# A streaming-encoder step on one core: the order of work at the end of the HGRN levels and around the expert gather

## The chip, the cores and the metric
One Trainium2 chip, one of its cores. The metric is the device time of one execution in microseconds, median of several runs; lower is better. All data are float32.

## What is computed
One layer over 320 tokens, 256 of a prompt and 64 of a sample, model width 2048. In short, with `h = adaLN(RMSNorm(x))`:
```
proj = h @ w_in                        # split into z, xbc, dt, hq, hf, hi, hgate, u
A: Mamba-2 SSD      B: HGRN2 (4 heads, key 128, value 128)      C: S5 diagonal SSM
x += gt1 * (concat(A, B, C) @ w_out)
x += gt2 * hmoe(adaLN(RMSNorm(x)))     # top-1 group, top-2 of its 8 experts, 32 experts of width 256
y = RMSNorm(x)
```
The part that the first half of the change touches is the chunkwise gated recurrence of B, in chunks of 64 tokens:
```
b = cumsum(log f)                       # in the chunk
intra = (q . k . exp(b_t - b_s), s <= t) @ v
inter = (q * exp(b)) @ S
kd = k * exp(b_last - b)
S = S * exp(b_last) + kd^T @ v
```
The second half sits where `hmoe` starts: router logits, top-1 group, softmax weights, and rows of `h` fetched for each expert.

## The kernel before
Five engines run own instruction streams, tied by semaphores; every step is laid out by hand, and within an engine all is in order. A list PLAN, made at build time by `make_plan` (line 75), gives TensorE its order; ScalarE and VectorE walk ACT_PLAN, the same list with slightly moved items.

**First 610 us.** TensorE multiplies `w_in` (17 chunks of 256 columns behind the first three, each 2 MB, two groups of 16 matmuls, line 1101) and `w_ada` (line 1000). SyncE loads the chunks into a ring of four slots as TensorE frees them (line 417). Between these "bulk" groups stand the small steps of S5 and of HGRN. HGRN takes two heads at once (hp = 0, 1). `hg_prep` makes log f and its running sum `hb`. Then seven levels: in level 0 the diagonal, in levels 1 to 6 blocks of 32 down to 1 tokens. A level is two subtractions into `hE` on VectorE (lines 1840, 1841), an exponential on ScalarE (line 799), two products into `hq_` and `hk_` (lines 1844, 1845), 12 small matmuls (line 1207) and, one level later, a masked sum into `hAT` by `hg_take` (lines 1828, 1830).

Behind the levels stands `hg_kd` (lines 801 and 1847). VectorE takes the last level's scores with `hg_take(hp, 6)`, sets a small element as a signal (line 1850), ScalarE writes exp(b) over `hE` (line 803), VectorE makes `hq_ = q * exp(b)` (line 1852), copies the last column of each chunk (line 1854), writes b_last - b into `hE` (line 1855), ScalarE takes its exponential (line 805), VectorE multiplies by k (line 1857), and TensorE turns the result (line 1219). For hp = 0 the plan has on TensorE: level 6, `ada 19,0`, the turning, `in 14,1`. For hp = 1: level 6, `in 18,0`, the turning, `ada 23,0`. On VectorE, between level 6 and `hg_kd(0)`, stands a convolution step (lines 1926, 1928), and on ScalarE the taking of a group of `in 14` out of PSUM (lines 743, 744). `hg_state` and `hg_out` (line 1234) follow, the latter with `hq_` as an operand.

**610 to 805 us.** SSD, the output projection (lines 1134, 1388), the second norm.

**805 to 860 us.** ScalarE makes h (line 702), TensorE the logits (line 1403), and turns h back into rows in 12 groups of four transposes (line 1418; PSUM banks 4 to 7, so a group from the fifth on needs the copy four before it). VectorE runs the routing in some 30 tiny steps (2095 to 2139), hands `rt_expo` over at 2133, then makes the mask `Mk` (2139) that TensorE ranks (line 1426; behind the twelve groups in its order), takes the ranks (2150 to 2157), lets TensorE place tokens (1434) and writes the row numbers `slot_rows` (2165). ScalarE waits for `rt_expo`, does two small exponentials (917, 918), copies the twelve groups (924), then stores all rows of h to DRAM in two transfers (928, 929). GpSimd waits for `slot_rows` and the stores, then gathers the rows of the first pair of experts (634). TensorE turns these (1450), VectorE copies them (2197), and `hidden(0)` starts (1463).

**860 to 1366 us.** 16 pairs of experts. SyncE loads gate and up weights in halves as TensorE is done with a half (line 459), 12 MB a pair in all with the down weights; VectorE, ScalarE and TensorE form the activation and the down product (1487). Then the rows are gathered, weighed, normed and stored.

Of the kernel before, what the change touches and what calls it, by code (L numbers as in the profile page):

```python
# [24 lines left out]
P = 128  # L25
# [3 lines left out]
T = TP + TS  # L29
# [156 lines left out]
def build(nc, a, o):  # L186

    ctx = ExitStack()
    with ctx:
# [70 lines left out]
        hAT = ar(2944, 384)  # L260
        vn = ar(3328, 768).rearrange("p (h q k) -> p h q k", h=2, q=3)
# [231 lines left out]
        def _(pool):  # L493
# [128 lines left out]
            pool.wait_ge(S("h2_stored"), 32)  # L622
# [28 lines left out]
        def _(act):  # L651
# [144 lines left out]
            def hg_level(hp, lv):  # L796
                if lv:
                    act.wait_ge(S("hg_expo"), 6 * hp + lv)
                    st(s.activation(hE, hE, ACT.Exp), "hg_exp")

            def hg_kd(hp):
                act.wait_ge(S("hg_expo2"), 2 * hp + 1)
                st(s.activation(hE, hb, ACT.Exp), "hg_exp2")
                act.wait_ge(S("hg_expo2"), 2 * hp + 2)
                st(s.activation(hE, hE, ACT.Exp), "hg_exp2")
# [110 lines left out]
            act.wait_ge(S("rt_expo"), 1)  # L916
            st(s.activation(rt[:, 16:28], rt[:, 16:28], ACT.Exp))
            st(s.activation(rt[:, 240:243], rt[:, 240:243], ACT.Exp), "rt_exp")

# [7 lines left out]
            act.wait_ge(S("act_rows"), 12)  # L927
            act.dma_start(h2_dram[0:TP].rearrange("(j p) d -> p j d", p=P), hn[:, 0:2, :]).then_inc(S("h2_stored"), 16)
            act.dma_start(h2_dram[TP:T], hn[0:TS, 2, :]).then_inc(S("h2_stored"), 16)
# [49 lines left out]
        def _(pe):  # L979
# [6 lines left out]
            pe.wait_ge(S("setup_taken"), 1)  # L986
            def sum_squares(b, count, tag):
                for i in range(count):
                    pe.wait_ge(S("squares"), NORM[tag] + i + 1)
                    for q in range(2):  # L990
                        last = mm(bank(b, T), ones[:, :], sq[:, i % 2, q * T:q * T + T],
                                  start=(i == 0 and q == 0), stop=(i == count - 1 and q == 1))
                    last.then_inc(S("squares_used"), 1)
# [198 lines left out]
            def hg_level(hp, lv):  # L1192

                it = 7 * hp + lv
                if lv == 0:
                    pe.wait_ge(S("hg_k"), hp + 1)
                    q_, k_ = (flat[:, (x + 2 * hp) * T:(x + 2 * hp + 2) * T] for x in (HQ, HF))
                else:
                    pe.wait_ge(S("hg_qk"), 6 * hp + lv)
                    q_, k_ = hq_, hk_  # L1200
# [33 lines left out]
            def hg_out(hp):  # L1234
                pe.wait_ge(S("hg_S"), NCH * (hp + 1))
                pe.wait_ge(S("hg_sc_used"), 7 * (hp + 1))

# [272 lines left out]
            pe.wait_ge(S("act_rows"), 12)  # L1510
            for g_ in range(4):
                turn_x(0, g_, 0)
# [68 lines left out]
        def _(dve):  # L1581
# [265 lines left out]
            def hg_kd(hp):  # L1847
                q_, k_ = (flat[:, (x + 2 * hp) * T:(x + 2 * hp + 2) * T] for x in (HQ, HF))
                hg_take(hp, 6)
                st(v.memset(small[:, 60:61], 0.0), "hg_expo2")  # L1850
                dve.wait_ge(S("hg_exp2"), 2 * hp + 1)
                st(tt(hq_, q_, hE, MUL))
                e3, b3 = (t.rearrange("p (n r) -> p n r", r=CH) for t in (hE, hb))
                st(v.tensor_copy(small[:, 80:90].unsqueeze(2), e3[:, :, CH - 1:CH]))
                st(tt(e3, bc(b3[:, :, CH - 1:CH], [P, 10, CH]), b3, SUB), "hg_expo2")
                dve.wait_ge(S("hg_exp2"), 2 * hp + 2)
                st(tt(hE, k_, hE, MUL), "hg_kd")
                for h in range(2):
                    dve.wait_ge(S("hg_kd_turned"), 2 * hp + h + 1)
                    b4 = bank(6 + h, 384).rearrange("p (q k) -> p q k", q=3)  # L1860
                    st(v.tensor_copy(kdn[:, h, 0:2, :], b4[:, 0:2, :]))
                    st(v.tensor_copy(kdn[0:64, h, 2, :], b4[0:64, 2, :]), "hg_kdn" if h else None)
# [337 lines left out]
            dve.wait_ge(S("h2_stored"), 32)  # L2200
# [128 lines left out]
```

## Time and profile before

| | |
|---|---|
| median of 3 runs | 1426.47 us (1426.3 to 1431.44) |
| the profiled execution | 1419.03 us, of which its span 1417.2 us |
| mean granted TensorE clock of the span | 0.925 |
| TensorE busy | 1186.0 us, 84% of the span |
| VectorE, ScalarE, GpSimd busy | 517.5, 195.9, 260.9 us |
| chain that ended last | PE 47%, DMA 27%, DVE 9%, POOL 9% |

The profile is of one execution. PE is TensorE, PEld its weight loads, DVE VectorE, ACT ScalarE, POOL GpSimd, SP SyncE. "L1219" is line 1219 of the kernel. "x32" counts instructions; one float32 matmul is two of them. "[4.14 <-DVE mem L1857]" is idle time of the engine ahead of the row and what ended it. The granted clock is a share of 2.4 GHz; it is 1.00 or 0.50 (1.2 GHz), and values between are means over a stretch.

### The profile page before, as it was taken

What the parts mean: (1) busy time and instruction counts of PE and PEld (TensorE: products, weight loads), DVE (VectorE), ACT (ScalarE), POOL (GpSimd) and SP (SyncE); (2) the same over time, 40 slices, a digit from 0 to 9 for tenths busy, and PEclk for the clock granted to TensorE, in tenths of its full rate; (3) what the DMA queues carried; (4) which work ended last, traced back from release to release, by engine and by line L of the source; (5) the groups of instructions that cost most, each with busy time, mean ns of one, the idle gap of its engine ahead of it and who ended that gap; (6) DMA issues with size and microseconds to landing.
All of it is one profiled execution on the core that took longest, in us unless ns stands there. A gap on an engine that the chain in (4) does not pass through costs nothing.

```text
span 1417.2 us, 14773 instructions
## 1 busy us (share of the span) xinstructions
PE 1186.0 (84%) x5922; PEld 641.6 (45%) x5922; DVE 517.5 (37%) x991; ACT 195.9 (14%) x319; POOL 260.9 (18%) x568
## 2 busy tenths in 40 slices
PE   4789999998998899989989868878878888877840
PEld 2345555654565565656657543323333333333310
DVE  2412476565454464435642362111112111111208
ACT  1302110100211311232210140000000000000003
POOL 4070188884000000011120000100000000010010
PEclk9899999999999899979999988998999999999975
DMA  9999477765766467432223446999999999999934
GB/s 338 374 351 366 144 272 261 273 228 195 236 232 227 142 234 262 154 95 89 90 75 119 152 160 235 418 421 420 412 416 397 405 402 411 402 410 400 420 155 133
DMA packets 140086, 387.02 MB, mean 273 GB/s; under 512 B 15211, under 2 KB 54501, under 8 KB 112558
## 3 DMA queue, kind: packets, MB, share of 16 engines
q1 hardware_dynamic: 132208, 361.91, 67.7%
q0 software_dynamic: 6528, 18.72, 3.8%
q10 hardware_dynamic: 1280, 5.42, 1.1%
q8 instruction: 49, 0.80, 0.2%
q14 instruction: 21, 0.17, 0.0%
HBM read 385.95 MB, written 23.13 MB: 289 GB/s over the span
## 4 chain that ended last, share of the span: by engine, by line
PE 47%; DMA 27%; DVE 9%; POOL 9%; SPq 3%; issue 3%; ACT 2%; POOLq 0%; DVEq 0%; ACTq 0%
DMA slot<-in_w_exp_up 22%; PE psum L1101 11%; PE psum L1463 11%; PE psum L1134 5%; PE psum L1388 5%; DMA slot<-in_w_ada 3%; PE psum L1000 3%; PE psum L1030 3%; POOL mem L558 1%; POOL sq L556 1%; POOL sq L559 1%; POOL mem L561 1%; POOL sq L560 1%; POOL sq L557 1%; SPq L443 1%
## 5 line engine op out<-in xcount | busy, mean ns | idle before, releaser
L1463 PE MATMUL psum<-slot,mem 128*64 128x512 f32 x1024 | 256.0, 659 | 66.8 <-DMA slot<-in_w_exp_up 65.9
L1101 PE MATMUL psum<-hT,slot 128*128 128x320 f32 (+1 forms) x1056 | 298.5, 442 | 0.0
L1101 PEld LDWEIGHTS psum<-hT,slot 128*128 128x128 f32 (+1 forms) x1056 | 199.0, 191 | 96.7 <-issue 21.5
L1463 PEld LDWEIGHTS psum<-slot,mem 128*64 128x64 f32 x1024 | 81.9, 151 | 232.0 <-issue 156.6
L2207 DVE TENSOR_TENSOR sq<-sq,psum 128x256 f32<-128x256 f32 x16 | 6.7, 422 | 328.1 <-ACT sq L935 328.1
L1487 PE MATMUL psum<-mem,sq 128*64 128x512 f32 x512 | 113.4, 595 | 8.3 <-issue 6.6
L1000 PE MATMUL psum<-slot,cT 128*8 128x512 f32 (+1 forms) x768 | 103.0, 647 | 20.7 <-DMA slot<-in_w_ada 20.7
L628 POOL DMA_INDIRECT moe_output<-mem,idx x16 | 16.2, 1010 | 481.8 <-ACT mem L939 481.8
L1134 PE MATMUL psum<-mem,slot 128*128 128x320 f32 x256 | 76.9, 458 | 0.0
L1388 PE MATMUL psum<-mem,slot 128*128 128x320 f32 x256 | 71.1, 441 | 5.4 <-DVE mem L2022 5.4
L1487 PEld LDWEIGHTS psum<-mem,sq 128*64 128x64 f32 x512 | 42.0, 137 | 69.5 <-issue 67.9
L1388 PEld LDWEIGHTS psum<-mem,slot 128*128 128x128 f32 x256 | 49.7, 195 | 26.4 <-issue 6.5
L1134 PEld LDWEIGHTS psum<-mem,slot 128*128 128x128 f32 x256 | 50.5, 201 | 24.6 <-issue 7.1
L935 ACT ACTIVATE sq<-psum 128x256 f32<-128x256 f32 x16 | 6.1, 383 | 340.2 <-PE psum L1463 340.2
L1450 PE MATMUL psum<-ident,mem 128*128 128x128 f32 x256 | 38.4, 285 | 17.4 <-DVE mem L2197 9.0
L1000 PEld LDWEIGHTS psum<-slot,cT 128*8 128x8 f32 (+1 forms) x768 | 17.3, 90 | 73.0 <-issue 67.9
L2197 DVE COPY mem<-psum 128x512 f32<-128x512 f32 x64 | 42.5, 684 | 9.5 <-PE psum L1450 9.5
L1450 PEld LDWEIGHTS psum<-ident,mem 128*128 128x128 f32 x256 | 29.1, 145 | 33.2 <-issue 30.9
L939 ACT ACTIVATE mem<-psum 128x1024 f32<-128x1024 f32 x16 | 16.4, 1023 | 161.8 <-PE psum L1487 161.8
L2220 DVE COPY mem<-psum 128x1024 f32<-128x1024 f32 x16 | 19.6, 1224 | 51.9 <-PE psum L1487 51.9
L634 POOL DMA_INDIRECT mem<-moe_input,idx x16 | 16.4, 1026 | 119.5 <-DMA moe_input<-mem 115.0
L1030 PE MATMUL psum<-hT,mem 128*128 128x320 f32 x128 | 37.3, 442 | 1.3 <-ACT hT L702 1.3
(448 smaller groups left out, 1259.7 us busy)
## 6 DMA issues: line engine op xcount, KB each, us to landing
slot<-in_w_ada SPq DMA_DIRECT2D x48, 2048.0 KB, 10.7
slot<-in_w_exp_gate SPq DMA_DIRECT2D x64, 1024.0 KB, 13.3
slot<-in_w_exp_up SPq DMA_DIRECT2D x64, 1024.0 KB, 16.4
mem<-in_w_exp_down SPq DMA_DIRECT2D x32, 2048.0 KB, 17.5
slot<-in_w_in SPq DMA_DIRECT2D x17, 2048.0 KB, 11.8
slot<-in_w_out SPq DMA_DIRECT2D x8, 2048.0 KB, 8.0
mem<-in_w_in SPq DMA_DIRECT2D x2, 2048.0 KB, 18.0
mem<-in_x_prompt ACTq DMA_DIRECT2D x1, 2048.0 KB, 12.1
```

Source lines behind the costliest of these rows:

```text
L634: pool.indirect_dma_start(xg[i % 2], None, h2_dram, bass.IndirectOffsetOnAxis(ap=slot_rows[:, i:i + 1], axis=0), bounds_check=T - 1, oob_i ...
L939: s.activation(ys[:, 1024:2048], psum[:, 3:5, :].rearrange("p b n -> p (b n)"), ACT.Copy)\
L1000: done = mm(psum[32 * c:32 * c + width, 2, :], cT[:, 8 * h + kk, lo:lo + width], w[:, kk, :], start=(first and kk < 4), stop=(last and kk ...
L1030: last = mm(bank(EARLY_BANK[e], T), w[:, k, q * P:(q + 1) * P], hT[:, k, :], start=(k == 0), stop=(k == KD - 1))
L1101: last = mm(psum[0:wd, grp % 2, 0:T], w[:, k, q * P:q * P + wd], hT[:, k, :], start=(k == 0), stop=(k == KD - 1))
L1134: last = mm(bank(grp % 2, T), w[:, k, q * P:(q + 1) * P], mixed[8 + k], start=(k == 4), stop=(k == 3))
L1388: last = mm(bank(4 + m % 4, T), w[:, k, q * P:(q + 1) * P], mixed[k], start=(k == 0), stop=(k == 7))
L1450: last = tr(bank(6 + g_ % 2, P, lo=q * P), xg[par][:, (4 * g_ + q) * P:(4 * g_ + q + 1) * P], ident[:, :])
L1463: last = mm(psum[rows_, 0, :].rearrange("p (w n) -> p w n", w=2), xe[i % 2][:, k, rows_], gate_up[h][:, :, k, :], start=(k == 0), stop=(k ...
L1487: last = mm(psum[rows_, 1 + n, :], aTT[:, f, rows_], dn[h][:, f, 512 * n:512 * n + 512], start=(f == 0), stop=(f == 1))
L2197: v.tensor_copy(xe[par][:, 4 * g_:4 * g_ + 4, :], bank(6 + g_ % 2).rearrange("p (k t) -> p k t", k=4))\
L2220: v.tensor_copy(ys[:, 0:1024], psum[:, 1:3, :].rearrange("p b n -> p (b n)")).then_inc(S("y_left"), 1)
```

## The change
In HGRN, exp(b) gets a buffer of its own, `hX`, and is made in level 2. In `hg_kd`, b_last - b is formed at once, and the take of level 6 and `q * exp(b)` come behind the decayed keys; `hg_qk` counts seven steps for each hp instead of six, and `hg_out` waits for the seventh. At the gather, the two exponentials of the gate move behind the twelve copies; each tile of rows is stored as soon as its four copies are done, in three transfers; and TensorE runs 18 matmuls of constants (`idle_work`) into bank 4 ahead of the turning of the first gathered rows.
```diff
+        hX = ar(7168, 640)
...
-            pool.wait_ge(S("h2_stored"), 32)
+            pool.wait_ge(S("h2_stored"), 48)
...
+                if lv == 2:
+                    if hp:
+                        act.wait_ge(S("hg_qk"), 7 * hp)
+                    st(s.activation(hX, hb, ACT.Exp), "hg_exp2")
 
             def hg_kd(hp):
-                act.wait_ge(S("hg_expo2"), 2 * hp + 1)
-                st(s.activation(hE, hb, ACT.Exp), "hg_exp2")
-                act.wait_ge(S("hg_expo2"), 2 * hp + 2)
+                act.wait_ge(S("hg_expo2"), hp + 1)
                 st(s.activation(hE, hE, ACT.Exp), "hg_exp2")
...
-            act.wait_ge(S("rt_expo"), 1)
-            st(s.activation(rt[:, 16:28], rt[:, 16:28], ACT.Exp))
-            st(s.activation(rt[:, 240:243], rt[:, 240:243], ACT.Exp), "rt_exp")
-
             for g_ in range(12):
...
-            act.wait_ge(S("act_rows"), 12)
-            act.dma_start(h2_dram[0:TP].rearrange("(j p) d -> p j d", p=P), hn[:, 0:2, :]).then_inc(S("h2_stored"), 16)
-            act.dma_start(h2_dram[TP:T], hn[0:TS, 2, :]).then_inc(S("h2_stored"), 16)
+                if kg == 3:
+                    act.wait_ge(S("act_rows"), g_ + 1)
+                    act.dma_start(h2_dram[j * P:j * P + n], hn[0:n, j, :]).then_inc(S("h2_stored"), 16)
+            act.wait_ge(S("rt_expo"), 1)
+            st(s.activation(rt[:, 16:28], rt[:, 16:28], ACT.Exp))
+            st(s.activation(rt[:, 240:243], rt[:, 240:243], ACT.Exp), "rt_exp")
...
+            def idle_work(b, count):
+
+                for _ in range(count):
+                    mm(bank(b, P), ones[:, :], ident[:, :], start=True, stop=True)
...
-                    pe.wait_ge(S("hg_qk"), 6 * hp + lv)
+                    pe.wait_ge(S("hg_qk"), 7 * hp + lv)
...
                 pe.wait_ge(S("hg_sc_used"), 7 * (hp + 1))
+                pe.wait_ge(S("hg_qk"), 7 * (hp + 1))
...
             pe.wait_ge(S("act_rows"), 12)
+            idle_work(4, 18)
...
-                hg_take(hp, 6)
-                st(v.memset(small[:, 60:61], 0.0), "hg_expo2")
+                e3, b3, x3 = (t.rearrange("p (n r) -> p n r", r=CH) for t in (hE, hb, hX))
+                st(tt(e3, bc(b3[:, :, CH - 1:CH], [P, 10, CH]), b3, SUB), "hg_expo2")
                 dve.wait_ge(S("hg_exp2"), 2 * hp + 1)
-                st(tt(hq_, q_, hE, MUL))
-                e3, b3 = (t.rearrange("p (n r) -> p n r", r=CH) for t in (hE, hb))
-                st(v.tensor_copy(small[:, 80:90].unsqueeze(2), e3[:, :, CH - 1:CH]))
-                st(tt(e3, bc(b3[:, :, CH - 1:CH], [P, 10, CH]), b3, SUB), "hg_expo2")
+                st(v.tensor_copy(small[:, 80:90].unsqueeze(2), x3[:, :, CH - 1:CH]))
                 dve.wait_ge(S("hg_exp2"), 2 * hp + 2)
                 st(tt(hE, k_, hE, MUL), "hg_kd")
+                hg_take(hp, 6)
+                st(tt(hq_, q_, hX, MUL), "hg_qk")
...
-            dve.wait_ge(S("h2_stored"), 32)
+            dve.wait_ge(S("h2_stored"), 48)
```

## Rows read from the trace of the kernel before

**Rows 1.** The page, busy time, share of the span, instructions.
```profile
PE 1186.0 (84%) x5922; PEld 641.6 (45%) x5922; DVE 517.5 (37%) x991; ACT 195.9 (14%) x319; POOL 260.9 (18%) x568
```
**Rows 2.** Windows, the expert stage: length, busy by engine (instructions), clock, DMA share, GB/s.
```profile
900.00:1300.00 400.00, 327.84 (x1510) 130.76 (x1512) 69.62 (x110) 16.89 (x24) 24.33 (x24) 0.92 1.00 410
```
**Rows 3.** The chain that ended last, in order of time: start, length, what.
```profile
859.17 13.97 PE psum L1463 x64
...
1348.37 8.81 PE psum L1463 x32
```
**Rows 4.** Waits of TensorE, 440 to 860 us, the longest: total, times, longest.
```profile
PE psum L1450 <- DMA mem<-moe_input,idx: 6.9, 1, 6.9
```
**Rows 5.** Timeline, end of the HGRN levels of hp = 0.
```profile
435.00 1.28 DVE L1928 SCALAR_TENSOR_TENSOR mem<-mem,parT,sq 128x256 f32<-128x256 f32 x4
...
438.26 0.22 ACT L744 ACTIVATE mem<-psum 128x64 f32<-128x64 f32 x1
438.52 1.90 PE L1000 MATMUL psum<-slot,cT 128*8 128x512 f32 x16
...
440.02 0.74 ACT L803 ACTIVATE mem<-mem 128x640 f32<-128x640 f32 x1 [1.54 <-DVE small L1850]
...
443.68 0.83 DVE L1857 TENSOR_TENSOR mem<-mem 128x640 f32<-128x640 f32 x1 [0.93 <-ACT mem L805]
...
444.56 1.42 PE L1219 MATMUL psum<-ident,mem 128*128 128x128 f32 x6 [4.14 <-DVE mem L1857]
```
**Rows 6.** The chain in order of time, around both turnings of the decayed keys.
```profile
445.99 9.74 PE psum L1101 x32
...
551.82 8.81 PE psum L1101 x32
560.63 0.65 PE psum L1219 x6
```
**Rows 7.** Timeline of ScalarE behind the exponential of level 2, hp = 1.
```profile
521.19 0.74 ACT L799 ACTIVATE mem<-mem 128x640 f32<-128x640 f32 x1 [7.85 <-DVE mem L1841]
```
**Rows 8.** Timeline, row turning and routing.
```profile
827.47 1.97 PE L1418 MATMUL psum<-ident,hT 128*128 128x128 f32 x16
...
833.79 2.56 ACT L924 ACTIVATE mem<-psum 128x512 f32<-128x512 f32 x5
...
834.53 5.01 PE L1418 MATMUL psum<-ident,hT 128*128 128x128 f32 x32 [5.10 <-ACT mem L924]
...
835.35 0.26 DVE L2139 TENSOR_TENSOR sq<-sq 128x96 f32<-128x96 f32 x1
...
840.70 0.23 DVE L2150 COPY sq<-psum 128x64 f32<-128x64 f32 x1 [3.06 <-PE psum L1426]
...
846.78 0.18 DVE L2165 CAST idx<-mem 128x32 uint32<-128x32 f32 x1
...
847.14 0.59 PE L1439 MATMUL psum<-mem,ones 128*128 128x3 f32 x2 [1.13 <-DVE mem L2166]
```
**Rows 9.** The chain in order of time, store and gather.
```profile
840.83 8.42 DMA moe_input<-mem
...
850.18 4.28 DMA mem<-moe_input,idx
...
854.60 1.94 PE psum L1450 x8
```
**Rows 10.** Timeline, TensorE at full clock: eight transposes; eight 128-column matmuls.
```profile
873.06 1.09 PE L1450 MATMUL psum<-ident,mem 128*128 128x128 f32 x8
...
1105.87 2.05 PE L1507 MATMUL psum<-ident,modT 128*128 128x128 f32 x16
```
**Rows 11.** Windows of 1 us around the gather, columns as in Rows 2.
```profile
837.00:838.00 1.00, 1.00 (x10) 1.00 (x9) 0.57 (x3) 0.74 (x3) 0.00 (x0) 0.87 0.00 0
...
844.00:845.00 1.00, 1.00 (x8) 0.85 (x8) 0.00 (x0) 0.00 (x0) 0.00 (x0) 0.55 0.94 393
...
857.00:858.00 1.00, 1.00 (x8) 0.96 (x6) 0.48 (x2) 0.00 (x0) 0.00 (x0) 0.63 0.00 0
```

## The prediction
> **What bounds the kernel now.** First the page: TensorE is busy for 84% of the span, the others far less [rows 1]. That is an average, so I read it by stage. In the expert stage, 900 to 1300 us, TensorE is busy for 328 of 400 us while the DMA engines are at a share of 1.00 and 410 GB/s [rows 2]: there the weights set the pace. The chain in order of time says when this begins. `hidden(0)` starts at 859.17, and the first weights of the next pair are asked for when its first half is done, 7 us later; the last half ends at 1357.2 [rows 3]. So work ahead of 859.17 can still be saved, and what is saved there moves the whole transfer stage; inside it nothing is gained by a faster TensorE.
>
> Ahead of it, the list of TensorE's waits between 440 and 860 us is what to look at: no transfer of weights is in it, and its longest is for the gathered rows, 6.9 us [rows 4]. The timeline has the two stalls that the change aims at. At the end of the levels of hp = 0 TensorE waits 4.14 us for the decayed keys [rows 5]; around the routing it waits 5.10 us for ScalarE's first row copies [rows 8], and the store and gather follow in the chain [rows 9].
>
> **Decayed keys, hp = 0.** TensorE is done with `ada 19,0` at 438.52 + 1.90 = 440.42 and turns the keys only at 444.56 [rows 5]. The chain between is: take of level 6, signal, exp(b) at 440.02, product, last columns, difference, exponential, product with k at 443.68. After the change the difference needs only `hb`, so VectorE makes it when the convolution ends, at 436.3 [rows 5]. ScalarE takes its exponential behind the PSUM copies that end at 438.26 + 0.22 = 438.48; with 0.74 each for the exponential [rows 5] and 0.05 of handing over it is done at 439.3. The product, 0.83, is done at 440.2, ahead of the 440.42. The margin is 0.2 us, thin but positive. Saved: 444.56 - 440.42 = 4.1 us.
>
> The stall also costs clock. With it, turning and the next group take 1.42 + 9.74 = 11.2 us; for hp = 1, where TensorE does not wait, the turning takes 0.65 and a like group 8.81, together 9.5 [rows 5, 6]. So 1.7 us more, and 5.8 us in all. The bounds of this term are 4.1 (the clock falls anyway) and 5.8.
>
> What goes behind the keys is hidden: take, sum and `q * exp(b)` are about 2 us of VectorE and must be done before `hg_out`; the copies of the turned keys come 1 us behind the turning and TensorE has a group of 8.81 us [rows 6] ahead of `hg_state`. If that group were not there, these 2 us would show. For hp = 1 TensorE passes from the group to the turning without a gap, 551.82 + 8.81 = 560.63 [rows 6], so nothing is to be had: 0. The additional exponential, 0.74 for each hp, is issued behind level 2's own; ScalarE's next work there comes after 7.85 us of idling [rows 7]: 0. Its wait for `hg_qk` (hp = 1) is met long before; behind it in the queue stands only the next PSUM copy. `hg_out`'s new wait is met ahead of the group that TensorE does before `hg_state`: 0. The signal and its hand-over go too, on no path that is left.
>
> **Gate exponentials behind the row copies.** Now the first four groups are turned at 827.47 + 1.97 = 829.44, but ScalarE copies only from 833.79, when `rt_expo` has come, and TensorE's other eight run from 834.53 to 839.54 [rows 8]. The ranking stands behind them, so VectorE, with its next operand ready, idles 3.06 us until 840.70 [rows 8]. After the change the copies start at 828.1, take 12 x 0.51 (2.56 for five [rows 8]) and two issues of about 0.5, and the turnings end at about 834. `Mk` is there at 835.35 + 0.26 = 835.6 [rows 8], the ranking takes a good microsecond, and VectorE goes on when its own work is done, at 837.64. Saved on the routing chain: 3.0 us; `slot_rows` comes at 843.96 instead of 846.96. Next in line is VectorE itself, so no more than 3.06 is to be had. The exponentials, with a table load, come at about 836 to 838; their reader, VectorE's weights, stands at 848 - 3 = 845. Behind ScalarE's wait for `rt_expo` stands only the first SiLU of the experts: 0.
>
> **Rows stored by tile.** Now 2 MB and behind them 0.5 MB are issued; the latter, issued at 840.83, lands 8.42 later, at 849.25; the gather starts at 850.18, 0.93 behind it [rows 9]. In the new order the stores are issued at about 830.7, 833.2 and 835.9, when the DMA engines are idle (share 0.00 [rows 11]). Were the last to take the whole 8.42 us, it would land at 844.3; with a fifth of the bytes left it will be well ahead of the 843.96. So the row numbers come last: gather at 843.96 + 0.93 = 844.9, landed 4.28 later [rows 9], TensorE could turn at 849.3. Against 854.60 [rows 9] that is 5.3 us. The third issue costs ScalarE 0.5 us, hidden under the wait for `Mk`.
>
> **Constant matmuls.** TensorE's last small step ends at 847.14 + 0.59 = 847.73 [rows 8], so at 844.7 in the new order, and the 18 matmuls start there. Their price is not in the stage, but eight matmuls of this shape take 2.05 us at full clock [rows 10], 0.256 each, 4.6 for 18: till 849.3, just when the rows land. At half clock eight transposes take 1.94 against 1.09 [rows 9, 10], a ratio of 1.78, so 0.456 each and 8.2 us: till 852.9. Which clock? Before the change TensorE resumed at 834.53 and the second 837 to 838 reads 0.87; it resumed at 854.60 and 857 to 858 reads 0.63 [rows 8, 9, 11]. As only 0.50 and 1.00 occur, the rises are at 837.3 and 857.7, 2.7 and 3.1 us after the work resumed. Short bursts did not hold it: it fell at about 844.1 amid work (0.55 [rows 11]). The new order has such pauses too, so I take 2.9 us at half clock (6.4 matmuls) and 11.6 x 0.256 = 3.0 at full: 5.9 us, till 850.6. The filler then holds the turning by 1.3 us (bounds 0 and 3.6).
>
> The Trainium skill ("TensorE: Matmul & The Clock Gate", Part 1, "Wait — 56ns, not 53.3ns?") has back-to-back matmuls of 128 columns at 107 ns with the array cold and 56 warm, a ratio of 1.9. By it an all-cold filler would be an estimated 8.8 us, the hold 4.2 instead of 3.6, and the sum 0.6 less in that case; it speaks for the first rival below, and the trace's 1.78 roughly agrees.
>
> What it buys: the turning runs at full clock, 8 transposes 0.85 us faster [rows 9, 10]. Turning to `hidden(0)` took 859.17 - 854.60 = 4.57; it will take 3.7. So `hidden(0)` starts at 850.6 + 3.7 = 854.3: 4.9 us earlier (bounds 1.7, all half: 852.9 + 4.57 = 857.5; and 6.2, all full: 849.3 + 3.7 = 853.0).
>
> **Sum.** 5.8 + 4.9 = 10.7 us. The profiled execution took 1419.03 (span 1417.2 and 1.8 around it): 1408.3. It is 7.4 us below the median of the runs shown, 1426.47; nothing in the change depends on where those 7.4 lie, so I take the same saving off the median: 1415.8. A measurement of this kernel can tell about 0.5%, 7.1 us, from no change.
>
> **Rival 1: the filler holds the rows.** It runs at half clock throughout and TensorE, in order, turns at 852.9. For it: 844 to 845 reads 0.55 just where the clock would be needed [rows 11]. Against: the filler is itself gapless work, and both rises came within 3.1 us of such. 5.8 + 1.7 = 7.5: 1419.0, at the edge of what can be told.
>
> **Rival 2: the HGRN gain is given back.** TensorE comes 5.8 us earlier to each later step up to 805 us; if a load of the ring or a partner engine has its own time, the stall reappears there. Against: no weight transfer in 420 us of waits [rows 4]; the partners start from TensorE's own results. For: a margin of only 0.2 us at the keys. Then 4.9 are left: 1421.6, no change.
>
> **Rival 3, slower: TensorE becomes the bound of the expert stage.** It has 400 - 328 = 72 us of room in 400 [rows 2], over 12 pairs 6 us a pair. The new start shifts its waits against the clock's falls; should it run at half clock for over 6 us of work more in each pair (mean clock from 0.92 to about 0.75), each pair is drawn out. One microsecond a pair over 15 pairs costs 15: 1426.5 - 10.7 + 15 = 1430.8. It decides from 0.7 us a pair. For it: the clock is below 1 in the stage already. Against: the pattern of waits is made by the transfers and returns in each pair.
>
> **How the numbers follow.** Forecast 0.66, rival 1 0.14, rival 2 0.14, rival 3 0.04, both parts without effect 0.02. The forecast's own bounds are 4.1 + 4.9 = 9.0 and 5.8 + 6.2 = 12.0, so 1414.5 to 1417.5. Three executions of the old kernel lie 5 us apart, so below I go to 1410; above, the range takes in rivals 1 and 2: 1422. Faster by over 0.5% (below 1419.3): 0.66 and half of rival 1, 0.73. Within 0.5%: the other half, rival 2 and the 0.02, 0.23. Slower: 0.04.
>
> **What would show it.** In the new profile: TensorE turns the keys of hp = 0 directly behind `ada`, with no wait at L1219 and the group behind it at 8.81; the copies at L924 start within 1 us of the first turning; VectorE's wait ahead of the ranks is gone; the gather starts under 1.2 us behind `slot_rows` and not behind a store; clock rises inside the filler; `hidden(0)` starts 10 to 11 us earlier and the DMA stage keeps its length. I am wrong if the filler ends over 2 us behind the landing of the rows, if TensorE shows a new wait between 440 and 805 us, or if the expert stage grows.

## Result and profile after

| | before | after |
|---|---|---|
| median, six runs each | 1427.33 us (1426.01 to 1431.44) | 1415.11 us (1410.4 to 1420.39) |
| ratio, 95% interval | | 0.9924 (0.9907 to 0.9941) |
| profiled execution: span | 1417.2 us | 1408.6 us |
| mean granted clock | 0.925 | 0.922 |

The kernel is faster by 0.76%, 10.8 us by the ratio, with an interval of 2.4 us to either side; the two medians lie 12.2 us apart. The forecast was 1415.8 in place of 1426.47, 10.7 us. The span of the profiled execution went down by 8.6.

What bounds the kernel is as before. The page of the changed kernel, busy time of each engine, answers to [rows 1]:

```profile
PE 1190.3 (85%) x5958; PEld 644.9 (46%) x5958; DVE 517.0 (37%) x989; ACT 195.8 (14%) x319; POOL 261.4 (19%) x568
```
The window of the expert stage of the changed kernel, columns as in [rows 2]:
```profile
890.00:1290.00 400.00, 325.70 (x1508) 130.51 (x1506) 70.12 (x110) 17.29 (x25) 24.37 (x24) 0.91 1.00 410
```

The DMA share is 1.00 and the rate 410 GB/s in both, so the gain should lie ahead of the stage. At the keys of hp = 0 the chain in order of time of the changed kernel (start, length, what) has no wait left; compare [rows 5, 6]:

```profile
438.72 1.83 PE psum L1008 x16
440.55 0.81 PE psum L1227 x6
441.36 8.62 PE psum L1109 x32
```

L1227 is the turning, formerly L1219. The timeline of the changed kernel (start, busy time, engine, line) shows why it is not late: the difference (L1860) is formed when the convolution ends, the exponential (L808) behind ScalarE's copies, the product (L1864) ends 0.3 us before the turning.

```profile
436.43 0.83 DVE L1860 TENSOR_TENSOR mem<-mem 128x640 f32<-128x640 f32 x1
...
438.51 0.73 ACT L808 ACTIVATE mem<-mem 128x640 f32<-128x640 f32 x1
...
439.34 0.83 DVE L1864 TENSOR_TENSOR mem<-mem 128x640 f32<-128x640 f32 x1 [1.87 <-ACT mem L808]
...
440.49 0.87 PE L1227 MATMUL psum<-ident,mem 128*128 128x128 f32 x6
```

The routing, in the timeline of the changed kernel, answers to [rows 8, 9]:

```profile
821.68 3.71 PE L1427 MATMUL psum<-ident,hT 128*128 128x128 f32 x32
...
822.38 2.07 ACT L923 ACTIVATE mem<-psum 128x512 f32<-128x512 f32 x4 [4.87 <-PE psum L1427]
...
829.44 0.49 ACTq L928 DMA_DIRECT2D moe_input<-mem  x1
...
831.89 0.22 DVE L2159 COPY sq<-psum 128x64 f32<-128x64 f32 x1
...
834.14 3.73 PE L1443 MATMUL psum<-rows,sq 128*64 128x32 f32 x24 [2.50 <-DVE sq L2166]
...
838.64 0.18 DVE L2174 CAST idx<-mem 128x32 uint32<-128x32 f32 x1
...
839.45 6.49 PE L993 MATMUL psum<-ident,ones 128*128 128x128 f32 x36
...
839.71 1.12 POOL L635 DMA_INDIRECT mem<-moe_input,idx  x1 [110.83 <-DVE mem L2175]
...
845.78 1.04 PE L1459 MATMUL psum<-ident,mem 128*128 128x128 f32 x8
```

ScalarE copies (L923) 0.7 us behind the first turning; VectorE takes the ranks (L2159) without the idling of 3.06 us; the gather (POOL L635) is released by VectorE's row numbers, not by a store; the filler (L993) ends when TensorE turns (L1459). `hidden(0)` starts at 849.4 against 859.2.

Executions differ by up to 4 us in when they reach the levels of hp = 0, so from here on I compare lengths of stretches, each the difference of two starts read from the timelines. The **lead** is from the last small matmul of level 6 to the turned keys; the **middle** from there to the last logits matmul (the last of the small ones that turn the logits and add their bias, L1408 before, L1417 after); the **gather** from that matmul to the first weight load of the second pair; the **rest** from that load to the end of the span. The column "rows" is when VectorE starts to write the row numbers, counted from the last logits matmul. For before: `hidden(0)` at 31.85 and the load 7.12 later, 38.97.

| kernel | lead | middle | rows | gather | rest |
|---|---|---|---|---|---|
| before | 6.19 | 382.76 | 19.46 | 38.97 | 550.9 |
| after | 1.98 | 381.05 | 17.11 | 35.00 | 552.1 |
| hgrn_only | 1.98 | 385.86 | 19.47 | 38.98 | 552.3 |
| gather_only | 6.19 | 385.69 | 17.11 | 35.48 | 551.9 |
| no_fill | 1.98 | 385.93 | 17.11 | 35.97 | 552.2 |
| fill36 | 1.98 | 380.48 | 17.10 | 39.05 | 552.5 |
| two_stores | 1.98 | 380.47 | 17.10 | 35.03 | 552.4 |
| exps_first | 1.98 | 387.08 | 21.32 | 38.83 | 550.9 |
| take_first | 4.10 | 384.04 | 17.11 | 35.47 | 552.4 |
| clock_hold | 6.19 | 385.30 | 21.32 | 41.85 | 551.4 |
| spread_fill | 1.98 | 385.75 | 15.77 | 32.19 | 555.4 |
| more_fill | 1.98 | 377.50 | 15.84 | 31.97 | 555.0 |
| silu_early | 1.99 | 383.86 | 17.11 | 35.00 | 550.4 |
| more_fill_silu | 1.98 | 378.18 | 15.84 | 32.02 | 551.5 |

Of the kernels whose time is not told below, one execution each: `fill36` 1414.06, `two_stores` 1412.72, `exps_first` 1420.39, `take_first` 1417.16, `clock_hold` 1424.06; executions of one kernel lie up to 13 us apart (`before`: 1421.9 to 1434.6 in 20), so their verdicts rest on the stretches alone.

From before to after: -4.2 in the lead, -1.7 in the middle, -4.0 in the gather, +1.2 in the rest and +0.1 in the start, together -8.6. A single middle is a poor witness, though: in the kernels that turn the keys at 1.98 and have no filler in the middle it lies anywhere from 380.5 to 387.1. That goes with the granted clock. Summed over the middle, TensorE was at 0.50 for 51 us in `before`, `after`, `fill36` and `two_stores` (middles of 380.5 to 382.8), for 58 us in `hgrn_only`, `gather_only`, `no_fill`, `spread_fill` and `silu_early` (383.9 to 385.9), and for 65 us in `exps_first` (387.1); `take_first` and `clock_hold` lie between, with 55 us (384.0) and 61 us (385.3). The -1.7 of this one pair of profiles is therefore no measure of what the change did to the clock. That is why the parts were timed as well.

### The profile page after: what moved, and what is told of

It reads as the page before. It is cut to its first block, busy times and chain, and to the rows that moved or that the text cites. A ratio compares the mean times of both kernels' runs of the same rounds, so it can differ in the third digit from the quotient of the medians.

```text
span 1408.6 us, 14842 instructions
## 1 busy us (share of the span) xinstructions
PE 1190.3 (85%) x5958; PEld 644.9 (46%) x5958; DVE 517.0 (37%) x989; ACT 195.8 (14%) x319; POOL 261.4 (19%) x568
## 4 chain that ended last, share of the span: by engine, by line
PE 49%; DMA 26%; DVE 9%; POOL 9%; SPq 3%; issue 3%; ACT 2%; POOLq 0%; DVEq 0%; ACTq 0%
DMA slot<-in_w_exp_up 21%; PE psum L1109 11%; PE psum L1472 11%; PE psum L1397 5%; PE psum L1142 5%; DMA slot<-in_w_ada 3%; PE psum L1008 3%; PE psum L1038 3%; PE psum L1496 2%; POOL mem L559 1%; DMA mem<-in_w_exp_down 1%; POOL sq L557 1%; POOL sq L560 1%; POOL mem L562 1%; POOL sq L561 1%
## 5 line engine op out<-in xcount | busy, mean ns | idle before, releaser
L1008 PE MATMUL psum<-slot,cT 128*8 128x512 f32 (+1 forms) x768 | 103.5, 650 | 20.8 <-DMA slot<-in_w_ada 20.8
L1008 PEld LDWEIGHTS psum<-slot,cT 128*8 128x8 f32 (+1 forms) x768 | 17.2, 90 | 73.0 <-issue 68.1
L1459 PE MATMUL psum<-ident,mem 128*128 128x128 f32 x256 | 37.1, 278 | 13.2 <-DVE mem L2206 10.9
L1459 PEld LDWEIGHTS psum<-ident,mem 128*128 128x128 f32 x256 | 27.9, 140 | 29.0 <-issue 25.7
L635 POOL DMA_INDIRECT mem<-moe_input,idx x16 | 16.5, 1028 | 115.4 <-DVE mem L2175 110.8
## 6 DMA issues: line engine op xcount, KB each, us to landing
slot<-in_w_ada SPq DMA_DIRECT2D x48, 2048.0 KB, 10.2
slot<-in_w_in SPq DMA_DIRECT2D x17, 2048.0 KB, 11.7
```

The source lines that it names most:

```text
L635: pool.indirect_dma_start(xg[i % 2], None, h2_dram, bass.IndirectOffsetOnAxis(ap=slot_rows[:, i:i + 1], axis=0), bounds_check=T - 1, oob_i ...
L1008: done = mm(psum[32 * c:32 * c + width, 2, :], cT[:, 8 * h + kk, lo:lo + width], w[:, kk, :], start=(first and kk < 4), stop=(last and kk ...
L1459: last = tr(bank(6 + g_ % 2, P, lo=q * P), xg[par][:, (4 * g_ + q) * P:(4 * g_ + q + 1) * P], ident[:, :])
```

## Experiments

### The two parts alone
`hgrn_only` has the HGRN part of the diff and the old gather; `gather_only` the reverse.
```diff
 hgrn_only, against the changed kernel
+            act.wait_ge(S("rt_expo"), 1)
+            st(s.activation(rt[:, 16:28], rt[:, 16:28], ACT.Exp))
+            st(s.activation(rt[:, 240:243], rt[:, 240:243], ACT.Exp), "rt_exp")
             for g_ in range(12):
...
-                if kg == 3:
-                    act.dma_start(h2_dram[j * P:j * P + n], hn[0:n, j, :]).then_inc(S("h2_stored"), 16)
...
+            act.dma_start(h2_dram[TP:T], hn[0:TS, 2, :]).then_inc(S("h2_stored"), 16)
...
-            idle_work(4, 18)
 gather_only, against the changed kernel
-                    st(s.activation(hX, hb, ACT.Exp), "hg_exp2")
...
+                st(s.activation(hE, hb, ACT.Exp), "hg_exp2")
...
+                hg_take(hp, 6)
+                st(v.memset(small[:, 60:61], 0.0), "hg_expo2")
+                dve.wait_ge(S("hg_exp2"), 2 * hp + 1)
+                st(tt(hq_, q_, hE, MUL))
...
                 st(tt(hE, k_, hE, MUL), "hg_kd")
-                hg_take(hp, 6)
-                st(tt(hq_, q_, hX, MUL), "hg_qk")
```


> The HGRN part of the change alone; gate exponentials, stores and gather as in the kernel before, no constant matmuls. Theory 1 (the two parts add up: 5.8 us at the keys of hp = 0, 4 us at the gather): TensorE turns the keys directly behind ada, hidden(0) starts near 859.2 - 5.8 = 853.4, the time is 0.996 of before (1421.5 against 1427.3). Theory 2 (the HGRN gain is given back before the expert stage and all of the gain is the gather's): hidden(0) at 859 +- 0.5, ratio 1.000.

> The gather part alone; HGRN as in the kernel before. Theory 1: the wait of 4.1 us at the keys is back, hidden(0) starts 4.0 us earlier than before, at 855.2, ratio 0.997. Theory 2 (the gather brings all): hidden(0) near 849.4, ratio 0.992.

Measured: `hgrn_only` 1421.35 us, ratio 0.9958 (0.9939 to 0.9977); `gather_only` 1421.88, ratio 0.9957 (0.9940 to 0.9975), both against 1426.96. Two gains of about 6 us, which add up to 12.1 where the whole change has 10.8 with an interval of 2.4 to either side. The HGRN gain is not given back as a whole; its interval, 3.3 to 8.7 us, holds the wait alone (4.2) as well as wait and clock (5.8). The expected starts of `hidden(0)` were absolute times of one execution and can't be compared; the stretches can: the lead is 1.98 and 6.19, the gather 38.98 and 35.48. For `gather_only` 4 us were expected and 6.1 came, with an interval of 3.6 to 8.6 that holds both; `exps_first` below has a possible reason for more than 4.

### take_first: the order in front of the keys
```diff
+                hg_take(hp, 6)
                 st(tt(e3, bc(b3[:, :, CH - 1:CH], [P, 10, CH]), b3, SUB), "hg_expo2")
...
                 st(tt(hE, k_, hE, MUL), "hg_kd")
-                hg_take(hp, 6)
```


> The whole change, but the take of level 6 stands ahead of the difference for the decayed keys again; exp(b) stays in its own buffer and q * exp(b) behind the keys. Theory 1 (each step of the chain counts with its length): take 1.2, difference 0.9, exponential 0.8, product 0.9 behind level 6; the keys are turned 4.1 us behind the last small matmul of level 6, against 2.0 in the changed kernel and 6.2 before: half of the gain. Theory 2 (moving exp(b) away is enough): 2.0 to 2.5 us.

Measured: 4.10. The timeline of `take_first` has the wait back at half its length:
```profile
443.41 0.87 PE L1227 MATMUL psum<-ident,mem 128*128 128x128 f32 x6 [2.05 <-DVE mem L1865]
```
Theory 1 holds to a tenth: the chain is a sum of its steps. Half of the gain comes from the separate buffer for exp(b), with which signal, exponential and product leave the chain; the other half comes from moving the take of level 6 behind the keys.

### clock_hold: the wait without its clock
The kernel before and, in TensorE's wait, constant matmuls.
```diff
             def hg_kd(hp):
 
+                if hp == 0:
+                    idle_work(3, 15)
                 pe.wait_ge(S("hg_kd"), hp + 1)
```


> The kernel before, with 15 constant matmuls in TensorE's wait for the decayed keys of hp = 0 and nothing else. Theory 1 (1.7 us of the 5.8 are the clock that falls in the wait): the keys are still turned 6.2 us behind level 6, but turning and the group behind it take 9.5 us instead of 11.2. Theory 2 (the clock falls for another reason): 11.2 as before.

Measured, in the chain in order of time of `clock_hold`, where [rows 5, 6] have 1.42 and 9.74:
```profile
443.65 0.88 PE psum L1226 x6
444.52 8.62 PE psum L1106 x32
```
9.50 us with the wait in place, so at this place the 1.7 us are the clock. But they do not last. In `hgrn_only`, `no_fill`, `exps_first`, `spread_fill` and `more_fill` the clock falls a little later, behind `hg_state`, with no wait of TensorE there longer than 0.8 us; in the chain of `hgrn_only` the second group behind the keys is the one that pays:
```profile
442.31 0.80 PE psum L1227 x6
443.11 8.62 PE psum L1109 x32
...
455.45 10.50 PE psum L1109 x32
```
10.50 against 8.81 is the same 1.7. That is five of the ten kernels that turn the keys at 1.98. In the other five (`after`, `two_stores`, `fill36`, `silu_early`, `more_fill_silu`) that group takes 8.81, and the clock falls further on, around `hg_out`, and stays at 0.50 for longer than before. The chain of the kernel before, at the group behind the wait for `hg_prep(1)`:
```profile
489.57 1.54 PE psum L1189 x6
491.12 9.37 PE psum L1101 x32
500.49 1.81 PE psum L1000 x13
```
The chain of the changed kernel, the same place:
```profile
484.52 1.54 PE psum L1197 x6
486.06 10.20 PE psum L1109 x32
496.26 1.83 PE psum L1008 x16
```
From the turned keys to the last of these rows (L1000, L1008) it is 500.49 - 444.56 = 55.9 us before and 496.26 - 440.49 = 55.8 after: of the 1.7 us, some 0.15 are left. Read from the timelines, the same stretch is 55.6 to 57.5 us in the ten kernels, apart from the two `more_fill` ones (54.7 and 53.8), and 55.8 to 57.3 in the four that turn the keys later; `clock_hold` itself, which changes nothing but the clock in the wait, has the 55.8 of the kernel before. So without a filler further on, no profile keeps the clock's share for 60 us; the wait's 4.2 us are what stays. What decides where the clock falls again was not found.

### exps_first and two_stores: which reordering moves the gather
```diff
 exps_first, against the changed kernel
+            act.wait_ge(S("rt_expo"), 1)
+            st(s.activation(rt[:, 16:28], rt[:, 16:28], ACT.Exp))
+            st(s.activation(rt[:, 240:243], rt[:, 240:243], ACT.Exp), "rt_exp")
             for g_ in range(12):
...
-            st(s.activation(rt[:, 16:28], rt[:, 16:28], ACT.Exp))
-            st(s.activation(rt[:, 240:243], rt[:, 240:243], ACT.Exp), "rt_exp")
 two_stores, against the changed kernel
-                if kg == 3:
-                    act.wait_ge(S("act_rows"), g_ + 1)
-                    act.dma_start(h2_dram[j * P:j * P + n], hn[0:n, j, :]).then_inc(S("h2_stored"), 16)
+            act.wait_ge(S("act_rows"), 12)
+            act.dma_start(h2_dram[0:TP].rearrange("(j p) d -> p j d", p=P), hn[:, 0:2, :]).then_inc(S("h2_stored"), 16)
+            act.dma_start(h2_dram[TP:T], hn[0:TS, 2, :]).then_inc(S("h2_stored"), 16)
```


> The whole change, but the two gate exponentials stand ahead of the twelve copies again. Counted from the last logits matmul: the copies start at 8.2 us, row turning ends near 14, the row numbers come at 19.5 instead of 17.1, the gather at 20.6 instead of 18.2. Theory 1 (the order of the exponentials is what brings the gather forward): the first load of the second pair is issued 2.4 us later than in the changed kernel, at 37.4 against 35.0. Theory 2 (the split of the stores brings it): under 1 us later.

> The whole change, but the rows of h stored in two transfers behind all twelve copies, as in the kernel before. Counted from the last logits matmul: the stores are issued at about 7.3 us, the last lands 8.42 us later, at 15.7; the row numbers are written at 17.1. Theory 1 (behind the reordering the row numbers come last): the gather starts at 18.2 as in the changed kernel, the split brings nothing. Theory 2 (the split is what removes the store from the chain): the gather starts 0.5 us or more later.

`exps_first` loses 3.8 us in the gather, not 2.4. Its timeline:
```profile
834.97 0.21 ACT L920 ACTIVATE mem<-mem 128x12 f32<-128x12 f32 x1 [8.73 <-DVE mem L2142]
...
836.19 6.20 PE L1427 MATMUL psum<-ident,hT 128*128 128x128 f32 x32 [5.09 <-ACT mem L927]
```
The eight late groups take 6.20 us where [rows 8] have 5.01: in the kernel before the clock came back in the middle of them (at 837.2), here it is at 0.50 from before they start until 841.4, 1 us before they end. Placing, later, takes 3.73 us against 3.05. Row numbers come at 21.3, as in `clock_hold`, whose gather part is the old one too. So the old order has at least two lengths, 38.97 and 41.85, and my one profile had the shorter. This would fit the 6 us of `gather_only`; how often each comes was not counted.

`two_stores` changes nothing: rows at 17.10, gather 35.03. In the timeline of `two_stores` the last store is issued 10 us before the row numbers, and it lands 2.5 us before the gather starts:
```profile
830.79 0.50 ACTq L928 DMA_DIRECT2D moe_input<-mem  x1
...
840.69 0.18 DVE L2174 CAST idx<-mem 128x32 uint32<-128x32 f32 x1
841.76 1.12 POOL L635 DMA_INDIRECT mem<-moe_input,idx  x1 [111.53 <-DVE mem L2175]
```
Once the exponentials stand behind the copies, the split by tile is worth nothing; their place is what counts.

### no_fill and fill36: the constant matmuls
```diff
 no_fill, against the changed kernel
-            idle_work(4, 18)
 fill36, against the changed kernel
-            idle_work(4, 18)
+            idle_work(4, 36)
```


> The whole change without the 18 constant matmuls. Theory 1 (the filler holds the landed rows by 1.7 us and gives back 1.1 in a faster turning): rows landed at 844.1 in the time of the changed kernel, eight plus eight transposes at half clock as before, 4.6 us to hidden(0), which starts at 848.7 against 849.4; the clock is back before it. Time within 1 us of the changed kernel, rather below. Theory 2 (the filler is needed): the turning is too short to bring the clock back, the first half of hidden(0) takes 2 to 7 us more than its 7, and the first load of the next pair is issued at 858.5 or later against 856.5; time 2 us or more above the changed kernel.

> The whole change with 36 constant matmuls instead of 18. Theory 1 (TensorE in order, the filler is already the last to end): the 18 more run at full clock, 0.25 us each, hidden(0) starts 4.5 us later, at 853.9. Theory 2 (the gathered rows come last and the filler hides behind them): under 2 us later.

Without the filler the rows are turned when they land, and `hidden(0)` starts 0.6 us earlier than with it (27.30 against 27.88), as theory 1 had it. But its first half takes 8.67 us instead of 7.12, so the load is asked for 1.0 us later. The chain in order of time of `no_fill` has it starting here:
```profile
855.43 15.52 PE psum L1472 x64
```
The windows of 1 us of `no_fill` (columns as in [rows 2]; the seventh number is the granted clock) show that the clock comes back only 3 us later:
```profile
858.00:859.00 1.00, 1.00 (x6) 0.42 (x4) 0.00 (x0) 0.00 (x0) 0.00 (x0) 0.70 0.00 0
```
Theory 1 missed that, and theory 2 overrated it. The time is 1417.8, ratio 0.9920 (0.9896 to 0.9944), which can't be told from 0.9924. So the filler is worth about 1 us, of which the time shows nothing certain.

With 36, `hidden(0)` starts 4.05 us later. The chain of `fill36`:
```profile
838.80 10.42 PE psum L993 x72
849.22 0.45 PE psum L1459 x4
```
18 more cost 10.42 - 6.36 = 4.06, 0.226 each at full clock. In the changed kernel the filler starts at 839.6, and its windows of 1 us put the clock's return just behind 844:
```profile
843.00:844.00 1.00, 1.00 (x6) 1.00 (x6) 0.15 (x1) 0.00 (x0) 0.00 (x0) 0.50 0.82 189
844.00:845.00 1.00, 1.00 (x11) 1.00 (x10) 0.00 (x0) 0.00 (x0) 0.00 (x0) 0.94 0.48 172
```
The filler ends at 845.95. So 1.8 us of it were at full clock, 8 matmuls, and the other 10 took 4.5 us: 0.45 each, twice 0.226. The Trainium skill ("TensorE: Matmul & The Clock Gate", Part 1) has 107 against 56 ns for matmuls of 128 columns in bf16, a ratio of 1.9; the trace agrees with that better than with the 1.78 that I had read from transposes.

### spread_fill and more_fill: the clock held where it pays
```diff
 spread_fill, against the changed kernel
+            idle_work(0, 7)
             pe.wait_ge(S("routed"), 1)
...
+            idle_work(0, 9)
             pe.wait_ge(S("routed"), 2)
...
+            idle_work(0, 3)
             pe.wait_ge(S("routed"), 4)
...
-            idle_work(4, 18)
+            idle_work(4, 15)
 more_fill, beside these
+                    idle_work(3, 17)
                     pe.wait_ge(S("hg_normed"), 2)
...
             pe.wait_ge(S("bulk_evac"), ALL_GROUPS)
+            idle_work(0, 17)
...
+            idle_work(1, 14)
             pe.wait_ge(S("router_loaded"), 64)
```


> The whole change with the constant matmuls spread over the waits of the routing: 7 ahead of the ranking, 9 ahead of the placing of tokens, 3 ahead of the last small step, 15 instead of 18 in the gather's wait. Theory 1 (what keeps the gather late is the half clock in the placing, 3.7 us, and in the filler): the clock stays full, placing takes about 2.1 us, row numbers at 15.5 us behind the logits instead of 17.1, rows are turned as they land, at 20.9 instead of 24.3, the first load of the second pair at 31.6 instead of 35.0; time 3.4 us below the changed kernel. Theory 2 (small matmuls do not hold the clock, the fillers only stand in the way): row numbers at 17 to 18, load at 35 or later, time as the changed kernel or above.

> As spread_fill, and constant matmuls in three earlier waits of TensorE: 17 ahead of hg_prep for hp = 1 (wait of 4.7 us), 17 ahead of the last output matmuls (5.4), 14 ahead of the logits (4.7). Theory 1: each wait ends as before and what follows runs at full clock: 1.4 + 1.0 + 0.5 us less between the keys and the logits, some 3 us below spread_fill. Theory 2 (a filler that meets half clock takes 0.36 to 0.43 us a matmul and outlasts its wait): TensorE is late at one or more of the three by 1 to 3 us and nothing is gained.

The chain of `spread_fill` has placing (L1445) at 2.39 us instead of 3.74, and a filler of 15 that ends 5.1 us after it started:
```profile
837.96 2.39 PE psum L1445 x24
841.47 0.39 PE psum L1451 x2
841.85 5.08 PE psum L993 x30
846.93 0.45 PE psum L1462 x4
```
Rows at 15.77, the load at 32.19: 2.8 us earlier than in the changed kernel, 3.4 expected. The time is 1412.85, ratio 0.9890 (0.9866 to 0.9913); the intervals of the two overlap. In this profile the rest is 3.3 us longer than the changed kernel's (555.4 against 552.1), which takes the 2.8 us of the gather back. `more_fill` is at 1407.91, ratio 0.9858 (0.9829 to 0.9888), clear of the changed kernel's 0.9924. Its group behind the wait for `hg_prep(1)` takes, in the chain, 0.87 + 8.62 = 9.5 where the changed kernel has 1.54 + 10.20 = 11.7 (shown above). The chain of `more_fill`:
```profile
488.74 0.87 PE psum L1198 x6
489.62 8.62 PE psum L1109 x32
```
The last output matmuls go from 70.4 to 68.7 us. Over the whole middle TensorE is at 0.50 for 31 us instead of 51. No filler held TensorE by more than 0.5 us behind its wait. `more_fill` beats both kernels. What it adds to the changed kernel is of two kinds, the spread fillers at the routing and three in earlier waits; `spread_fill` alone is not clear of the changed kernel, so how the gain divides between the two was not settled.

### silu_early: what the moved exponentials left behind
In the changed kernel the first pair of experts takes 27.3 us from `hidden(0)` to `hidden(1)`; before, it takes 24.3. The timeline of the changed kernel has a table load in front of the first SiLU:
```profile
863.44 1.28 ACT L937 ACT_TABLE_LOAD   x1 [31.75 <-PE psum L1472]
...
864.74 0.38 ACT L937 ACTIVATE sq<-psum 128x256 f32<-128x256 f32 x1
...
868.15 8.70 PE L1496 MATMUL psum<-mem,sq 128*64 128x512 f32 x32 [0.55 <-DVE sq L2223]
```
In the timeline of the kernel before there is none here:
```profile
873.16 0.38 ACT L935 ACTIVATE sq<-psum 128x256 f32<-128x256 f32 x1 [30.52 <-PE psum L1463]
...
876.58 7.09 PE L1487 MATMUL psum<-mem,sq 128*64 128x512 f32 x32 [0.55 <-DVE sq L2214]
```
With the exponentials in front, as in `exps_first`, this load stands right behind the issue of the last store, 31 us ahead of its use; in the changed kernel it stands behind the wait for TensorE's result of `hidden(0)`. Here the clock falls as well, and the down product takes 8.70 us against 7.09. The down weights are asked for 20.4 us behind the first load instead of 17.4, and the windows of 2 us of the changed kernel (columns as in [rows 2]) have a dip of the DMA share to 0.81 there:
```profile
878.00:880.00 2.00, 2.00 (x12) 0.73 (x10) 0.00 (x0) 0.00 (x0) 1.03 (x1) 1.00 0.81 270
```
```diff
             st(s.activation(rt[:, 240:243], rt[:, 240:243], ACT.Exp), "rt_exp")
+            st(s.activation(small[:, 59:60], small[:, 0:1], ACT.Silu))
```


> The whole change and one SiLU of a 128x1 element behind the two gate exponentials. In the changed kernel ScalarE's load of the SiLU table (1.28 us) stands in front of the first SiLU of the experts, where it ran hidden before; with the clock that falls behind it, the first pair takes 27.3 us from hidden(0) to hidden(1) against 24.3. Theory 1 (the load is exposed by the moved exponentials, and the down weights' issue 20.4 us instead of 17.4 behind the first load leaves the DMA engines a short gap): the first pair takes 24.3 again, the gap goes, the time is about 1 us below the changed kernel. Theory 2 (the stage is bound by transfers and the pair's length does not matter): 24.3, and no time.

> more_fill with the same early SiLU. Theory 1: about 1 us below more_fill, 1406 to 1407. Theory 2: the same as more_fill, 1408.

The pair takes 24.4 us again in both. The times: 1414.99, ratio 0.9932 (0.9912 to 0.9952), and 1405.13, ratio 0.9860 (0.9838 to 0.9882), against 0.9924 and 0.9858 without. The times show no difference, within about 3 us. The traces do show one. The last of the expert weights lands this far behind the first load of the second pair: 491.8 to 493.7 us in the six kernels that have the table load covered (before, `hgrn_only`, `exps_first`, `clock_hold` and these two), 492.3 and 492.9 in the two where it is exposed but no fall of the clock follows (`gather_only`, `take_first`, first pair 25.6), and 494.0 to 495.6 in the six where both come (first pair 26.7 to 28.8). The chain of the changed kernel, where this landing is 1350.73 - 856.52 = 494.2:
```profile
1330.30 20.43 DMA mem<-in_w_exp_down
```
The chain of `silu_early`, where it is 1354.19 - 862.42 = 491.8:
```profile
1333.33 20.86 DMA mem<-in_w_exp_down
```
So the transfers of the changed kernel take about 2 us longer than before, as theory 1 said, and theory 2 is not borne out by the traces. The rate says where most of it goes: in the changed kernel it is 270, 385, 307 and 389 GB/s in the four windows from 878 to 886 us, and some 420 around them, which makes an estimated 1.6 us of transfer; in the kernel before it is only 381 and 406 in the two windows of 888 to 892, an estimated 0.3 us. `silu_early` is at 426 in the window that corresponds to the dip. The other second was not followed.

## Why the prediction was right

The time came as forecast, and so did both mechanisms at their places: the wait at the keys is gone, and the row numbers release the gather. Two terms did not: the clock's share at the keys did not last, and the expert stage, put at no change, grew. By its steps:

- **Keys, wait: 4.1 forecast, 4.2 measured.** The sum of the chain held to a tenth, and the margin, forecast as 0.2 us, was 0.3. `take_first` confirms the method.
- **Keys, clock: 1.7 forecast, 1.7 measured at the place (`clock_hold`), some 0.15 left 56 us later** in the changed kernel. In five other profiles all of it was lost again 13 us behind the keys. The middle is 1.7 shorter in this pair of profiles, but by falls of the clock more than 120 us behind the keys (until there it is only 0.15 ahead), so that this agreement is luck. The lower bound of the term, 4.1, "the clock falls anyway", is what the profiles bear out.
- **hp = 1, the additional exponential, the new waits: 0 forecast.** Nothing of them shows in the chain.
- **Routing chain: 3.0 forecast, 2.35 measured.** VectorE does stop idling, 3.06 us; but placing went from 3.05 to 3.73 us, because the clock, which in the old profile fell in the midst of it (at 844.1), is now at 0.50 for all of it. The prediction left this term at its old price while it reckoned with a low clock 5 us later.
- **Stores by tile: not on the chain,** as forecast. The prediction put the release of the gather by the row numbers down to reordering and split together; `two_stores` shows that the reordering alone does it.
- **Filler: 5.9 us forecast, 6.36 measured, hold 1.3 forecast, 1.8 measured.** The price at half clock was 0.45, as taken; it lasted 4.5 us instead of 2.9. Its price at full clock was 0.226, not 0.256. Turning to `hidden(0)` took 3.5 instead of 3.7. The hold of 1.8 is the start of the turning against `no_fill`, 24.25 and 22.47 us behind the last logits matmul; in the changed kernel's own profile the rows landed late, 5.9 us behind the gather's issue where the other profiles have 4.1 to 4.5, so there they were held by no more than 0.3. The prediction's account lacked one thing: what the clock does to `hidden(0)` itself, 1.55 us, which is most of the filler's worth. Without it, its own numbers gave a filler that costs more than it brings: a hold of 1.3 us for 0.85 us in the turning.
- **`hidden(0)` 4.9 us earlier by the gather part: 4.0 in this profile**, 3.5 to 6.9 as compared with other profiles (35.0 and 35.5 against 39.0 and 41.9), 6.1 by the timed runs, with 3.6 to 8.6 as its interval.
- **Expert stage: no change forecast, 2.3 longer** to the last landing of weights (491.9 and 494.2); 1.1 of it came back behind the landing, and the rest is 1.2 longer. This is the one sign of being wrong in the list that did come about ("if the expert stage grows"). `hidden(0)` started 9.8 us earlier, where 10 to 11 were to show.
- **Rival 1** came about by half: the filler put the turning off by 1.8 of the possible 3.6. **Rival 2**, that the HGRN gain is given back, fell as a whole: 0.9958 alone. Its smaller form, that the clock's share is given back, is what the profiles show. **Rival 3**, a stage bound by TensorE, fell: the DMA share is 1.00 as before, and the stage grew by 2.3 us, not by 15.
- **Overlooked:** "Behind ScalarE's wait for `rt_expo` stands only the first SiLU of the experts: 0." The SiLU brought a table load of 1.28 us with it, out in the open. With the clock that falls behind it, the first pair is 3 us longer; about 2 us of this are in the transfers of the traces, and the timed runs can't tell it from nothing.

That the sum of 10.7 meets the measured 10.8 so closely is in part luck. In the profiles the lasting terms are 4.2 at the keys and 4.0 at the gather, less 1.2 in the rest: 7.0, with 1.7 more in the middle, most of it from falls of the clock far behind the keys, which differ by more than that from profile to profile. The timed runs give 6.0 and 6.1 for the parts, each within 2.7 us or so. They bear out that each part gains; they are too coarse to confirm its size.

## What to carry to other kernels

Where a chain of small steps on three engines stands in front of TensorE, its steps can be summed from the timeline, and what doesn't feed the result goes behind it. The clock that the wait costs, 1.7 us on a wait of 4.2 here, is to be taken as the upper bound of a term and not as part of the sum: follow the clock on to the next waits before counting it. A filler of constant matmuls pays for what runs behind it at full clock, not for the wait in which it stands, and each must be sized for half clock if it starts there. Short ones in seven waits gave 0.9858 against 0.9924 with one. When activations move, look where the table loads go.

## What was not expected of the hardware

- The granted clock fell to 0.50 behind `hg_state`, with waits of 0.8 us at most in front of it, in five of the ten kernels that turn the keys at 1.98 us; the group behind took 10.50 us instead of 8.81.
- The 24 small matmuls of the placing ran for 3.7 us at half clock and did not bring it back; the filler behind them took another 4.5 us to do so.
- The same order of instructions, the old one, gave rows at 19.46 us (`before`) or 21.32 us (`clock_hold`): 1.2 us in the eight late groups of turning and 0.7 in placing, both where less of the run was at full clock.
- TensorE's clock, brought back at one place, fell for longer at a later one: 0.50 for 10.2 us in the changed kernel, from 28.2 us behind the turned keys, where before it was 6.8 us from 30.9.
